# Router logits computed from the unnormed residual inside the output projection, with the norm of the expert input moved behind the ranking

## What is computed

```python
x = (x + gt1 * mix).astype(x.dtype)             # mix = merged @ w_out
h2 = rms_norm(x, g_norm2[l]) * (1.0 + sc2) + sh2
ffn = hier_moe(h2, w_group[l], b_group[l], w_router[l], b_router[l], ...)
x = (x + gt2 * ffn).astype(x.dtype)
...
def hier_moe(h, ...):
    grp_prob = softmax(hf @ w_group + b_group)        # 4 groups
    p_g, g_idx = lax.top_k(grp_prob, 1)
    exp_logits = (hf @ w_router + b_router)           # 16 experts, 4 of each group
    top_vals, e_idx = lax.top_k(sel_logits, 2)        # 2 experts of the chosen group
    y += silu(hf @ gate_e) * (hf @ up_e) * combine_e @ down_e
```

## Time and profile before

| | |
|---|---|
| median of 3 runs | 1890.35 us (1886.65 to 1897.05) |
| the profiled execution | 1897.58 us, its span 1895.8 us |
| PE busy | 1686.3 us, 89% of the span |
| DVE, ACT, POOL busy | 888.7, 495.2, 1003.5 us |
| mean granted PE clock | 0.93 |

### The profile page before, as it was taken

One profiled execution on the slowest core, in us unless ns is written; L12 is line 12 of the kernel. 1 busy time (PEld: TensorE's weight loads), 2 busy tenths in 40 slices (PEclk: granted clock), 3 DMA queues, 4 the chain that ended last, 5 costly groups with the idle time before them and its releaser, 6 DMA issues. The chain is left out here.

```text
span 1895.8 us, 20726 instructions
## 1 busy us (share of the span) xinstructions
PE 1686.3 (89%) x7778; PEld 1320.3 (70%) x7778; DVE 888.7 (47%) x1407; ACT 495.2 (26%) x941; POOL 1003.5 (53%) x945
## 2 busy tenths in 40 slices
PE   4999798998979969999998699999887699999995
PEld 2778676766758747778876487666564388888884
DVE  7684754298682471231215862765366521111114
ACT  2201222303241120123443412433444410000011
POOL 2756653355716526758870345222373157677672
PEclk8999898898999979999998799999897799999997
DMA  9355311024213022424544532101221012322211
GB/s 357 151 194 191 103 62 64 23 82 165 76 45 113 22 109 91 150 84 155 187 154 182 212 100 89 45 24 45 67 82 53 22 67 89 111 89 92 109 67 45
DMA packets 32695, 197.55 MB, mean 104 GB/s; under 512 B 3735, under 2 KB 7591, under 8 KB 10964
## 3 DMA queue, kind: packets, MB, share of 16 engines
q1 hardware_dynamic: 26040, 179.57, 26.0%
q10 hardware_dynamic: 5836, 14.03, 2.3%
q0 software_dynamic: 720, 2.62, 0.4%
HBM read 190.90 MB, written 7.66 MB: 105 GB/s over the span
## 5 line engine op out<-in xcount | busy, mean ns | idle before, releaser
L2429 POOL TENSOR_TENSOR b_wlo<-b_raw,b_whi 128x512 fp32r<-128x512 f32 x516 | 703.9, 1371 | 69.2 <-ACT b_whi L1469 34.0
L2423 POOL TENSOR_SCALAR b_whi<-b_raw 128x512 fp32r<-128x512 f32 x420 | 304.9, 726 | 787.3 <-PE ps L436 602.2
L434 PE MATMUL ps<-b_hhi,b_whi 128*128 128x512 f32 (+1 forms) x1128 | 456.6, 405 | 28.6 <-DVE b_hlo L1684 15.5
L435 PE MATMUL ps<-b_hlo,b_whi 128*128 128x512 f32 (+1 forms) x1128 | 448.4, 398 | 0.0
L436 PE MATMUL ps<-b_hhi,b_wlo 128*128 128x512 f32 (+1 forms) x1128 | 447.1, 396 | 0.0
L434 PEld LDWEIGHTS ps<-b_hhi,b_whi 128*128 128x128 f32 x1128 | 218.6, 194 | 92.8 <-issue 45.2
L436 PEld LDWEIGHTS ps<-b_hhi,b_wlo 128*128 128x128 f32 x1128 | 218.5, 194 | 46.6
L435 PEld LDWEIGHTS ps<-b_hlo,b_whi 128*128 128x128 f32 x1128 | 218.7, 194 | 44.5 <-issue 0.7
L1217 ACT ACTIVATE b_arena<-ps 128x512 f32<-128x512 f32 (+6 forms) x126 | 68.2, 545 | 400.0 <-PE ps L436 323.7
L434 PE MATMUL ps<-b_ahi,b_whi 128*128 128x512 f32 x416 | 166.2, 400 | 4.5 <-DVE b_alo L1684 3.6
L435 PE MATMUL ps<-b_alo,b_whi 128*128 128x512 f32 x416 | 163.7, 394 | 0.0
(11 more groups left out here) (322 smaller groups left out, 2098.6 us busy)
## 6 DMA issues: line engine op xcount, KB each, us to landing
b_raw<-in_stream SPq DMA_DIRECT2D x165, 1024.0 KB, 4.8
bias_near<-bias_vectors ACTq DMA_DIRECT2D x1, 2298.0 KB
b_x<-in_xT SPq DMA_DIRECT2D x1, 2048.0 KB, 13.6
b_x<-in_xT ACTq DMA_DIRECT2D x1, 2048.0 KB, 7.7
h_tokens<-b_y ACTq DMA_DIRECT2D x1, 2048.0 KB, 11.7
b_arena<-in_cw ACTq DMA_DIRECT2D x1, 2048.0 KB, 7.2
out<-b_x SPq DMA_DIRECT2D x8, 256.0 KB, 2.0
bias_compressed<-bias_vectors ACTq DMA_DIRECT2D x1, 1024.0 KB
```

The lines of the kernel that those rows point to most:

```text
L434: pe.matmul(o, ahi_, bhi_, start=start, stop=False)
L435: pe.matmul(o, ahi_, blo_, start=False, stop=False)
L2423: nc.gpsimd.tensor_scalar(whi[:, s, c], raw[:, r, c], 1.0, 1.0, ALU.mult, ALU.mult)\
L2429: nc.gpsimd.tensor_tensor(wlo[:, s, c], raw[:, r, c], whi[:, s, c].bitcast(F32), ALU.subtract)\
```

## The change

- Eight route steps are put into the output projection: as soon as X slice k is final, ACT makes the high part of X * gain (`hi_of` with `gain`), DVE the low part (`lo_of` with `gain`), and PE adds the slice's share to the logits (`route_step(k)`), one step behind the projection's slices. The split goes to the buffers ahi and alo.
- Ahead of the projection PE multiplies the shift with the router weights (16 products of one column); DVE lays the result on a diagonal (`route_bias`).
- After the norm factor, DVE multiplies the 20x512 logits by it (`rout`). PE turns them by 4 products with the identity and adds the shift's row by 4 products more, where it had 4 transposes.
- DVE forms h2 (8 slices) after `ranked`, ahead of the routing's small instructions, and ACT's high parts move behind its first exponential.
- The 8 halves of `h2_turned` go from before expert 0 to between its two pieces, in two PSUM banks of their own; `slots_filled` goes behind the second piece.

`linear_summed`, `by_tiles` and `by_rows` are added and called by nothing.

```diff
 PE
-            linear("wout", range(KD), KD, hhi, hlo, 0, "wout_read", "merged")
+            share_banks(side=[6, 7])
+            pe.wait_ge(sem("router_split"), 1)
+            o = open_bank("shift", "shift_read", "side")
+            for k in range(KD):
+                for n, w in enumerate((rhi, rlo)):
+                    ins = pe.matmul(o[0:20, 0:1], w[:, k, :].bitcast(F32), mod[:, 24 + k:25 + k],
+                                    start=k + n == 0, stop=k + n == KD)
+            mark(ins, "shift")
+            linear("wout", range(2), KD, hhi, hlo, 0, "wout_read", "merged")
+            logits = open_bank("router", "router_T", "side")
+            def route_step(k):
+                pe.wait_ge(sem("lo"), SPLITS["route"] + k + 1)
+                return three(logits[0:20, :], rhi[:, k, :], rlo[:, k, :], ahi[:, k, :], alo[:, k, :],
+                             k == 0, k == KD - 1)
+            route_step(0)
+            for m in range(2, KD):
+                linear("wout", [m], KD, hhi, hlo, 0, "wout_read")
+                route_step(m - 1)
+            mark(route_step(KD - 1), "router")
             norm_product("sum_h2", KD)
-            for k in range(KD):
-                pe.wait_ge(sem("lo"), SPLITS["h2"] + k + 1)
-                ins = three(o[0:20, :], rhi[:, k, :], rlo[:, k, :], hhi[:, k, :], hlo[:, k, :], k == 0, k == KD - 1)
-            h2_turned(0, 0)
             pe.wait_ge(sem("router_T"), 1)
+            pe.wait_ge(sem("route_bias"), 1)
             for T in range(ST):
-                ins = pe.transpose(o[:, T * 32:T * 32 + 20], rout[0:20, T * P:(T + 1) * P], ident[0:20, 0:20])
+                pe.matmul(o[:, T * 32:T * 32 + 20], rout[0:20, T * P:(T + 1) * P], ident[0:20, 0:20], start=True, stop=False)
+                ins = pe.matmul(o[:, T * 32:T * 32 + 20], ones[0:20, :], route_bias, start=False, stop=True)
-            h2_turned(0, 1)
-            h2_turned(1, 0)
-            h2_turned(1, 1)
...
-            for T in range(2, ST):
-                h2_turned(T, 0)
-                h2_turned(T, 1)
...
                 o = wide_first(keys, hhi, hlo, ["silu_read"] * 2 + ["eu_read"] * 2, None if e else "h2")
+                if e == 0:
+                    for T in range(ST):
+                        pe.wait_ge(sem("lo"), SPLITS["h2"] + KD)
+                        h2_turned(T, 0)
+                        h2_turned(T, 1)
+                wide_second(o, keys, hhi, hlo)
                 if e == 0:
                     slots_filled()
-                wide_second(o, keys, hhi, hlo)
 ACT
             for k in range(KD):
-                act.wait_ge(sem("wout_read"), k + 1)
+                hi_of("route", k, ahi[:, k, :], src=X[:, k, :], ready=("wout_read", k + 1), gain=gain[:, k:k + 1])
                 square_for("sum_h2", k, X[:, k, :])
             rstd_of("sum_h2", D)
-            for k in range(KD):
-                hi_of("h2", k, hhi[:, k, :], src=h2f[:, k, :], bias=mod[:, 24 + k:25 + k])
-            evacuate("router", rout[0:20, :], "router_T", src=ps[0:20, bank_of["router"], :])
             act.wait_ge(sem("route_max"), 1)
             run(nc.scalar.activation(gl_e, gl_e, ACT.Exp), "route_exp")
+            for k in range(KD):
+                hi_of("h2", k, hhi[:, k, :], src=h2f[:, k, :], bias=mod[:, 24 + k:25 + k])
 DVE
+            finished(dve, "shift")
+            run(V.tensor_scalar(route_bias, ident[0:20, 0:20], ps[0:20, bank_of["shift"], 0:1], None, ALU.mult),
+                "route_bias")
             for k in range(KD):
                 finished(dve, ("wout", k))
                 run(V.scalar_tensor_tensor(X[:, k, :], bank(("wout", k)), mod[:, 16 + k:17 + k], X[:, k, :],
                                            op0=ALU.mult, op1=ALU.add), "wout_read")
-                add_squares_behind("sum_h2", k)
+                if k >= 2:
+                    add_square("sum_h2", k - 1)
+                lo_of("route", k, alo[:, k, :], ahi[:, k, :], X[:, k, :], gain=gain[:, k:k + 1])
+            add_square("sum_h2", KD - 1)
             wait_rstd()
+            finished(dve, "router")
+            run(V.tensor_tensor(rout[0:20, :], ps[0:20, bank_of["router"], :], rstd[0:20, :], ALU.mult), "router_T")
...
             run(V.tensor_scalar(group_at[:, :], group4, float(MOE_PIECES), None, ALU.mult), "ranked")
+            h2_formed()
```

More of the change, by code:

```diff
@@ L1207, in hi_of @@
                 if bias is None:
-                    run(nc.scalar.activation(dst, src, ACT.Copy), "hi")
+                    run(nc.scalar.activation(dst, src, ACT.Copy, scale=gain), "hi")
                 else:
```

83 lines of the change are left out of this document (59 added, 24 removed).

## The result

| | before | changed |
|---|---|---|
| median | 1892.15 us (6 runs, 1886.65 to 1897.05) | 1903.91 us (6 runs, 1897.29 to 1911.12) |
| the profiled execution | 1897.58 us, span 1895.8 | 1897.44 us, span 1895.6 |
| PE busy | 1686.3 us | 1676.7 us |
| mean granted PE clock | 0.93 | 0.936 |

The ratio is 1.006, 95% interval 1.003 to 1.009: slower by 11.8 us, where 13.5 was predicted.

A forecast was written before the change was run, and what follows sets the result against it. PE bounds the projection and experts, with a serial chain between that leaves it nearly idle; -2.85 up to the ranking plus +16.4 to expert 1 gave +13.5 on 1890.35, so 1904 us, range 1889 to 1910.

The forecast's parts named there:

- shift products: Ahead of the projection: 32 records taking 3.8 to 5.6 us, in PE's idle time; +0.3 us, bounds 0 and +2.2.
- wait before route step 0: In the projection behind slices 0 and 1, PE waits for ACT's and DVE's split of slice 0: 2.0 to 2.9, taken +2.9 us.
- slow clock behind that wait: Projection after PE's wait before step 0: 1.2 GHz level, 9 matmuls 0.43 instead of 0.23 apart; +1.7 us, bounds 0 and 1.8.
- route steps 0 to 5: Router steps inside the output projection lengthen it by 6 x 3 x 0.24: +4.3 us.
- step 7 and norm product: Projection's end: step 7 fits PE's 3.51 us wait, 0; bounds -1.0 if busier PE keeps the norm product's clock, and +0.5.
- factor to logits: From norm factor ready to logits read: 15.55 us becomes 3.5, so -12.05 us, bounds 0.5 either way.
- logits to R: From logits read to R, the time at which the ranking is done (before: 692.79): nothing changes, 0.
- part one: Everything up to the end of the ranking: sum -2.85 us, bounds -4.4 to +3.0.
- part two: From ranking to expert 1: h2 formed first, small routing instructions stretched beside POOL, transposes waiting for route_diff; +16.4 us.
- the first: Rival, 27%: routing instructions not stretched beside POOL, route_diff ahead of its need; total +3.4 us, 1894 us.
- the second: Rival, 6%: routing unstretched and the clock and covers all go well, total -3.6 us, 1887 us.
- The third: Rival, 7%: worse; shift products overrun (+1.9), wide operations block fully (+2), slot comparisons late (+3): +20 us, 1910 us.

The follow-up runs named there:

- routing_first: Changed kernel with DVE's 27 small routing instructions straight behind the ranking and h2 formed only after them; median 1895.72 us, ratio 1.0005 to the kernel before.
- act_order: Changed kernel with ACT's wait for route_diff and second exponential behind all eight copies of turned h2 halves; median 1900.33 us, ratio 1.0043 to the kernel before.
- h2_early: Changed kernel with h2 and the scan formed ahead of the logits, ACT's high parts ahead of its first exponential; median 1899.64 us, one run.
- steps_behind: Changed kernel with all eight router steps behind the projection's last slice, none inside it; median 1902.41 us, ratio 1.0045 to the kernel before.
- turned_ahead: Changed kernel with ACT's route_diff wait behind its copies and the 32 transposes back ahead of expert 0's products; median 1900.46 us, one run.

## Why the prediction was right

The forecast came true: 1904 us against 1903.9, slower, by the mechanism that it named. That it hit to 0.1 us is luck. It added 13.5 us to 1890.35, the median of three runs; six runs gave 1892.15, 1.8 us more, and the loss was 11.8 in the medians and 11.1 in the stretch. So a start that was too low hid a sum that was too high. The steps, in the order of the sum:

| step | predicted | measured |
|---|---|---|
| shift products | +0.3 | 0 |
| wait before route step 0 | +2.9 | +2.83 |
| slow clock behind that wait | +1.7 | 0 |
| route steps 0 to 5 | +4.3 | +4.4 |
| step 7 and norm product | 0 (-1.0 to +0.5) | -1.2 |
| factor to logits | -12.05 | -12.76 |
| logits to R | 0 | +0.84 |
| part one | -2.85 | -5.9 |
| part two | +16.4 | +17.05 |
| sum | +13.5 | +11.1 |

- **Shift products.** The 32 records start 25 ns apart (0.05 us for two), not 118 or 175 as the nearest rows suggested, end 2.6 us before the projection can start, and cost nothing.
- **The wait and the clock.** The wait is as predicted. The slow stretch behind it did not come at all. The windows of PE at the projection's start and behind the wait say so:

```profile
606.68:609.68 3.00, 3.00 (x7) 0.52 0.02 5
622.23:625.23 3.00, 3.00 (x13) 1.00 0.00 0
```

After 2.56 us idle PE ran at the 1.2 GHz level, after 2.83 us idle at 2.4. I had taken the only row of such a wait for the rule. The length of the idle time alone doesn't tell. What stood just before it was different: ahead of 606.68 and in the earlier trace rows narrow products (1.0 us of one column, 1.1 us of 4 rows), ahead of 622.23 wide ones only. Which of this decides, these runs don't show. The bound 0 was in the range.
- **Steps 0 to 5.** The last slice is added to X at 56.14 us of the stretch (before 48.94): 7.2, less the wait of 2.83.
- **Norm product.** From that addition to the factor it took 5.75 us, before 6.96. The busier PE kept the clock (1.13 us for the product, before 2.08), 0.2 beyond the bound that I had given.
- **Factor to logits.** 665.13 to 667.92 is 2.79 us, and 12.76 saved is 0.2 beyond the bound of 0.5 around 12.05; I had priced the 16 narrow records by rows with wider ones.
- **Logits to R.** 5.47 us, before 4.63: the counts ran at the lower clock (1.87 us). This had been put at 0 without a bound: before, the transposes stood there and kept PE busy, and the change took them away. A cover that goes can take its clock with it; these two profiles fit that, and no run tests it alone.
- **Part two**, relative to R, predicted and measured: POOL 8.0 and 8.0; expert 0 10.9 and 11.1; first piece over 23.2 and 24.0; `route_diff` 35.0 and 35.0; second piece 37.5 and 37.4, over at 49.7 and 49.3; slot products done 54.4 and 54.4; expert 1 60.0 and 60.65. The 0.65 is the weights' product, 2.07 us at the lower clock (before 1.12), less 0.2 of wait behind it. That `route_diff` was met so closely is luck too: the 27 instructions began at R + 18.5 where I had 19.4, and took 16.5 us where I had 15.6.

Of the signs that were named ahead, two did not show: no slow stretch stood behind the first wait, and R came 5.9 us earlier, not 2 to 4. The wait between the pieces was 7.94 us, just under the 8 to 9 named. (One slip of adding stands in the chances: 0.85 of 0.60 and 0.07 are 0.58, not 0.57.)

The price of 0.65 us for each small instruction beside POOL was read from four rows and is what decided the case; routing_first, and the 16 fast ones of the same kind once POOL is idle, show POOL as the cause. Of the rivals, the first (27%: routing not stretched) falls with the window of 16.50 us, the second with it. The third named an overrun of the slots too early: it did not come in the changed kernel, but a wait of 1.18 us did as soon as act_order took the larger one away.

**The rule on the ports.** A slice of h2 beside POOL costs 0.98 + 1.63 to 1.67 = 2.7 us in every run that has whole slices there, 1.5 to 1.6 alone, and POOL pays as well: its part takes 1.05 + 1.60 us beside a slice and 0.62 + 1.27 without one; the small instructions last until POOL's instruction ends. The Trainium skill (SBUF — State Buffer, Who interferes with whom) lets a two-input DVE instruction and GpSimd exclude each other fully, which by an estimate from the durations alone would make the slice 0.75 + 0.75 + 0.62 + 1.27 = 3.4. For the small instructions the trace agrees (1.13 us, ended within 0.02 us of POOL's); for the wide ones the measurement decides, and they overlap in part. The word of the Trainium skill in the same section that on this chip reductions never contend is borne out: the reduction behind the scan took 0.29 us beside POOL in routing_first and 0.29 with POOL idle in h2_early.

**What stays open.** What wins or loses the higher clock after a wait of 1 to 3 us, or in a run of narrow products, is not settled by these runs; it was worth 0.8 to 2.4 us at four places (counts, weights' product, logits in steps_behind, slot products in act_order). And the order with the norm product ahead of the last router steps wasn't tried: in steps_behind the norm product starts 5.3 us behind the last addition to X, in the changed kernel 3.1.

## What to carry to other kernels

An instruction that waits on another engine should stand behind whatever on its own queue others wait for, unless it is surely ready: here a single 0.2 us exponential held PE for 7.9 us, and moving it gave 5.5 us back. Before work is moved, ask of each engine what the mover's neighbours are doing there: short DVE instructions with two SBUF inputs cost 0.2 us with POOL idle and 0.65 beside its splitting, so put them where POOL is idle and leave the wide ones, which stretch less in proportion (1.7 times against 3), for the crowded time. And when a long wait is removed, compute when the next one in line is due; here the chain behind had 8.3 us to spare where the wait gave back 9.1.

## What the runs showed of the hardware

- Products of one column with 20 columns of weights start 25 ns apart (32 records in 0.8 us).
- A wait of 2.83 us left PE at the 2.4 GHz level (the changed kernel at 622.23), one of 2.56 us was followed by the 1.2 GHz level (606.68).
- In the 40 slot products of 5 columns PE fell to the 1.2 GHz level while it was busy: about 3.6 us behind the last wide product in the changed kernel, about 2.3 us (1.18 of them a wait) in act_order, and not at all in turned_ahead, which did all 40 in 4.4 us.
- Short DVE instructions beside POOL's alternating copies and subtractions go three for each part of 1.94 us, at 1.13, 0.55 and 0.17 us; with POOL idle and the DMA engines at 226 GB/s each takes about 0.17.
- The same program's time moves by 20 us along with the clock that is granted, 1.34 us for each 0.001 of the mean. In the fourteen profiles the part ahead of the stretch varies by 14.3 us (602.4 to 616.7), the part behind it by 5.2.
